# Nine added GpSimd drains near the ends of five stages of a seven-stage transformer block

## The reference

```python
h = layer_norm(concat([meta, x]), ln_in_g, ln_in_b)
proj = h @ w_in                        # 8 + 2*2 + 3*8 heads of 64, and 8 forget logits
o_a = sliding_sink_attention(qa, ka, va, sinks, rel_bias)      # windows of 128 frames, 8 heads
o_b = forgetting_attention(qb, kb, vb, log_sigmoid(fb + b_f))  # causal, 8 heads
h = layer_norm(2 ** 0.25 * h + concat([o_a, o_b]) @ w_o, ln1_g, ln1_b)
ffn = hierarchical_moe(h, ...)         # 1 of 4 groups, 2 of its 8 experts, SwiGLU of width 512
out = layer_norm(2 ** 0.25 * h + ffn, ln2_g, ln2_b)[16:]
```

## Time and profile before

| what | value |
|---|---|
| median of 3 runs | 2470.27 us (2469.62 to 2470.92) |
| the profiled execution | 2470.16 us, of which its span is 2468.5 us |
| busy, share of the span | PE 89%, PEld 72%, DVE 69%, ACT 60%, POOL 13% |
| POOL instructions counted as busy | 429, 324.4 us |
| DMA packets from GpSimd's queue (q0) | 31648, 101.89 MB, 14.3% of 16 engines' span |
| granted TensorE clock, mean | 0.947 |

### The profile page before, as it was taken

One profiled execution on the slowest core, in us unless ns is written; L12 is line 12 of the kernel. 1 busy time (PEld: TensorE's weight loads), 2 busy tenths in 40 slices (PEclk: granted clock), 3 DMA queues, 4 the chain that ended last, 5 costly groups with the idle time before them and its releaser, 6 DMA issues. The chain is left out here.

```text
span 2468.5 us, 35853 instructions
## 1 busy us (share of the span) xinstructions
PE 2192.7 (89%) x11294; PEld 1786.4 (72%) x11294; DVE 1709.2 (69%) x3150; ACT 1489.7 (60%) x2262; POOL 324.4 (13%) x429
## 2 busy tenths in 40 slices
PE   6999999678699989999899993799999999999970
PEld 5788888555477777777778872687888888788860
DVE  5323231288588887888643336898999999899976
ACT  4323241176577676777643330777888888788856
POOL 0112111100000000000000000222222222222211
PEclk9999999889899999999999995899999999999985
DMA  6536252533341222222043323897887969999837
GB/s 197 177 107 198 102 183 81 152 79 96 109 116 32 53 67 66 62 69 75 20 139 136 137 110 136 298 376 242 275 291 214 302 203 363 321 296 304 270 73 289
DMA packets 220553, 420.61 MB, mean 170 GB/s; under 512 B 47912, under 2 KB 97144, under 8 KB 219288
## 3 DMA queue, kind: packets, MB, share of 16 engines
q1 hardware_dynamic: 187760, 316.08, 37.9%
q0 software_dynamic: 31648, 101.89, 14.3%
q10 hardware_dynamic: 1040, 1.31, 0.2%
HBM read 437.68 MB, written 86.39 MB: 212 GB/s over the span
## 5 line engine op out<-in xcount | busy, mean ns | idle before, releaser
L2425 DVE TENSOR_TENSOR moe_w_lo<-fetch_w_raw,moe_w_hi 128x1024 fp32r<-128x1024 f32 x376 | 435.5, 1218 | 14.3 <-ACT moe_w_hi L2354 14.0
L2354 ACT ACTIVATE moe_w_hi<-fetch_w_raw 128x1024 fp32r<-128x1024 f32 x376 | 369.1, 1053 | 70.8 <-PEq L96 32.4
L2479 PE MATMUL moe_ps_gu<-moe_w_hi,moe_xT_hi 128*128 128x512 f32 x736 | 293.8, 399 | 4.3 <-DVE moe_xT_lo L2436 4.2
L2481 PE MATMUL moe_ps_gu<-moe_w_hi,moe_xT_lo 128*128 128x512 f32 x736 | 289.3, 393 | 0.0
L2480 PE MATMUL moe_ps_gu<-moe_w_lo,moe_xT_hi 128*128 128x512 f32 x736 | 289.0, 393 | 0.0
L1434 ACT ACTIVATE fox_p_hi<-fox_ps_t 128x512 fp32r<-128x512 f32 (+4 forms) x352 | 181.0, 530 | 108.7 <-PE fox_ps_t L1574 107.7
L1501 DVE TENSOR_TENSOR fox_p_lo<-fox_ps_t,fox_p_hi 128x512 fp32r<-128x512 f32 (+4 forms) x352 | 211.0, 611 | 28.9 <-ACT fox_p_hi L1434 28.1
L1574 PE MATMUL fox_ps_t<-ident,fox_s 128*128 128x128 f32 (+1 forms) x1216 | 199.8, 279 | 29.6 <-ACT fox_s L1427 18.8
L2431 DVE TENSOR_TENSOR moe_d_lo<-fetch_d_raw,moe_d_hi 128x1024 fp32r<-128x1024 f32 x184 | 213.1, 1221 | 10.5 <-ACT moe_d_hi L2362 7.2
L1488 DVE CUSTOM_DVE_ANT_0 fox_s<-fox_ps_r,fox_ncum 128x512 f32<-128x512 f32 (+4 forms) x352 | 193.6, 569 | 20.8 <-PE fox_ps_r L1559 13.5
L1427 ACT ACTIVATE fox_s<-fox_s,fox_ntop 128x144 f32<-128x144 f32 (+5 forms) x192 | 173.3, 904 | 48.0 <-DVE fox_ntop L1496 47.6
(11 more groups left out here) (319 smaller groups left out, 4978.8 us busy)
## 6 DMA issues: line engine op xcount, KB each, us to landing
fetch_w_raw<-in_w_e_gate_dram SPq DMA_DIRECT2D x192, 512.0 KB
fetch_w_raw<-in_w_e_up_dram SPq DMA_DIRECT2D x192, 512.0 KB
fetch_d_raw<-in_w_e_down_dram SPq DMA_DIRECT2D x92, 1024.0 KB
ahead_raw<-in_w_in_dram SPq DMA_DIRECT2D x24, 1024.0 KB, 5.2
gates_wide<-in_x_dram SPq DMA_DIRECT2D x16, 512.0 KB
h<-gates_wide POOLq DMA_DIRECT2D x16, 512.0 KB, 3.3
gates_wide<-qT SPq DMA_DIRECT2D x32, 256.0 KB, 4.1
mix_h<-h SPq DMA_DIRECT2D x16, 512.0 KB, 3.7
```

The costliest lines, as they stand in the source:

```text
L2354: nc.scalar.activation(w_hi[:, k], w_raw[:, k].rearrange("p j n -> p (j n)"), ACT.Copy).then_inc(gu_high, 1)
L2425: nc.vector.tensor_tensor(w_lo[:, k], w_raw[:, k].rearrange("p j n -> p (j n)"), w_hi[:, k].bitcast(F32), ALU.subtract).then_inc(gu_split, 1)
L2479: nc.tensor.matmul(out, xT_hi[:, slot, k], w_hi[:, k, cols], start=k == 0, stop=False)
L2481: done = nc.tensor.matmul(out, xT_lo[:, slot, k], w_hi[:, k, cols], start=False, stop=k == KT - 1)
```

## The change

Nine calls of `nc.gpsimd.drain()` are added to GpSimd's programs, in five of the seven stages. A drain has no semaphore; it stands in GpSimd's order in front of the store named, and nothing else is moved.

```diff
@@ phase_project
                 for i in range(QK):
+                    if sb == SBS - 1 and i in (QK - 4, QK - 1):
+                        nc.gpsimd.drain()
                     store_chunk(sb, i)
@@ phase_window
+                if n in (TILES // 2, TILES - 1):
+                    nc.gpsimd.drain()
                 pool.wait_ge(o_ready, 2 * (n + 1))
@@ phase_mix
             def store(n, slot, use):
+                if is_tile(n, TILES - 2, TILES - 1):
+                    nc.gpsimd.drain()
                 pool.wait_ge(h1_scaled, n + 1)
@@ phase_combine
             def store(n, slot, use):
+                if n == TILES - 4:
+                    nc.gpsimd.drain()
                 pool.wait_ge(ready, n + 1)
```

## The result

| | before | after |
|---|---|---|
| median of the runs, us | 2470.6 (2469.62 to 2472.69, 4 runs) | 2449.79 (2448.41 to 2452.5, 4 runs) |
| the profiled execution, us; its span | 2470.16; 2468.5 | 2448.41; 2446.8 |
| GpSimd's drains at the ends of the seven stages, us in sum | 17.40 | 1.31 |
| mean granted clock | 0.947 | 0.949 |

The ratio is 0.9916 with an interval of 0.9899 to 0.9933: about 20.8 us less, where 15.6 were forecast.

A forecast was written before the change was run, and what follows sets the result against it. Seven serial stages end in barriers that wait for GpSimd's drains, 17.397 us in all. Ends gain 16.0 us, less 0.4 for first transfers: 15.6 off 2470.16 gives 2454.5; range 2451.5 to 2458.2, or to 2461 with the first rival.

The forecast's parts named there:

- The end drains: Ends of five stages: GpSimd's drains walk only transfers issued since the last drain, falling from 17.12 to 1.10 us.
- rival 2: Stage ends: semaphore clearing, not the drain, empties the list, so end drains keep their length; 2472 us, chance 0.08.
- rival 1: Stage ends: about 1.36 us is a fixed price of a drain behind any transfer; gain 10.3 us, 2459.8, chance 0.11.
- The cover of the added drains: Before the last stores: new drains' walks fit into GpSimd's idle waits and cost nothing; longest 6.5 us, in the projection.
- Rival 3: Added drains: walking beside working engines is far slower than in an empty stage; 2480 us at factor 5, chance 0.08.
- The rule of the Trainium skill: Added drains: GpSimd and VectorE lock each other out of a shared port, making the factor 5 and the result 2480.
- The first transfers behind a drain: Four last stores right behind new drains, on the path: each costs 0.1 us more, 0.4 us in all.
- The last stage: Only place without cover: tile 12's store up to 2.4 us late, the last two on time; cost taken as 0.
- it should move forward rigidly: After each barrier the next stage starts from its own loads and keys, fetched before, so it shifts without changing length.
- at most 2 to 3 us for the clock: Around 493 to 509: a pause 6.8 us shorter may leave fewer slow-clock microseconds; extra gain put into the lower bound alone.
- The prediction's low end, 2451.5: Range's lower bound: 2453.3 if only 46 ns of each drain remained and first transfers cost nothing, plus a little clock gain.

The follow-up runs named there:

- the second's 15.8: The changed kernel, unchanged, run again for more rounds against the kernel before: 2452.09 us against 2468.52, ratio 0.9936 (0.9920 to 0.9952).

## Why the prediction was right and where it failed

- **The end drains.** Right in mechanism and size: 16.07 us against 16.02. The drain in the middle empties the list, and the clearing of semaphores isn't needed for it, so rival 2 falls; the ends of 0.12 to 0.38 us rule out the floor of rival 1.
- **The cover of the added drains.** Right in its result; mis-sized in the walk. The prediction took 108 entries at 60 ns, 6.5 us, for the projection's first drain. It lasts 8.9 us from the end of the issue in front (452.87) to its own end (461.76), 82 ns for each: the 60 ns were 7.01/116, and at this price the end drain doesn't walk all 116. (The 49 ns of the experts were mis-sized in the same way.) Chunk 9 goes out at 462.25; it was due at 457.24 (the old 457.81, less 0.57 by which the stage ran ahead), so it is 5.0 us late instead of 2.2, and GpSimd is back in step at chunk 11 (468.12). That the walk runs beside the landing, as the prediction let it, holds there: the wait for chunk 9 is 9.38 us in all three profiles with this drain, though the landing in front of it takes 3.8, 3.5 and 3.2 us. Where the landing is the longer it doesn't quite hold, and a part of the walk stands behind the last landing: 0.41 us before tile 8 of the windows, 1.19 before tile 14 of the mixing, 0.54 in the last stage and 3.81 in the experts, the same to 0.01 us in three profiles each, and about half of what 9, 28, 12 and 92 entries make at 83 ns. The waits had room for it: in the experts 8.4 us of 13.20 were used.
- **Rival 3** falls with it: the walk costs 82 to 83 ns for each transfer beside working engines and 82 to 85 in the empty stage, a factor of 1; set against the prediction's 6.5 us it is 1.4, where 4.2 would have used up the gain. The rule of the Trainium skill that stood beside it ("SBUF — State Buffer", section "A bandwidth-pool intuition that's wrong (but worth ruling out)") would have made 32 us of the 6.5, as an estimate, 5 times as much; no run here shows that.
- **The first transfers behind a drain.** Mis-sized: 0.4 us was taken, and the stores behind the added drains take 0.53 to 0.55 us, and the two scatters 1.54 and 1.55, no more than before (0.539 and 1.543). Nothing was lost.
- **The last stage.** Right: tile 12 is late (3.2 us, 2.4 at most were forecast), the last two stores are on time.
- **The step that failed: "it should move forward rigidly", with at most 2 to 3 us for the clock.** The bodies of two executions differ by up to 6.2 us in the experts (853.3 to 859.5) and 4.1 in the windows (176.1 to 180.2), in kernels that do the same there. The prediction took the profile of before, 2470.16 us, as the level and three runs that agreed within 1.3 us as the spread; 27 runs spread over 11.2, with a median of 2468.52. That profile has the longest experts' body of ten, by two pauses of TensorE and the clock behind them; why VectorE was late there in some executions and not in others is open. The prediction's low end, 2451.5, held the walks and a little of the clock, and nothing for this. A second term was left out: the 0.83 us of the projection's last store.
- By the parts that come back, the change is worth 16.9 us; the first comparison's 20.8 and the second's 15.8 lie on either side. That the rest of the 20.8 is the spread of the bodies fits all ten profiles; with so few runs a systematic gain of a microsecond or two beside it is not excluded.

Some 1.05 us of walks is left in the five end drains, and no experiment points to a version that would be faster by an amount that can be measured.

## What to carry to other kernels

Where a stage ends with a barrier, look at the drain of each engine under the line that leaves it, not only at busy times: GpSimd's grows with the transfers that it has issued since its last drain, and a drain put where GpSimd waits anyway takes that off the path, if it fits into the wait: 82 to 85 ns for each transfer walked here, and up to half of that behind the landing of the store in front. Take the price from stages whose drains agree on it (three did, two did not). Count the gain by parts that come back from profile to profile, and put the spread of the remaining stages, from more than one profile of the kernel before, into the range.

## What the runs showed that was not expected

- Each transfer that GpSimd issued and that is still on the list costs its next drain 82 to 85 ns, long after it has landed, whether most of them moved 128 and 256 KB (projection, 82 and 83) or all 512 KB (last stage, 85), and whether the other engines work (82 and 83) or have finished.
- The list can shrink without a drain: 128 stores of the forgetting attention leave 1.365 us, 32 leave 0.229; in the projection 108 are walked by a drain before chunk 9 (8.9 us), but the end drain behind 116 takes 7.01.
- A TensorE pause of 3.14 us in the experts' loop goes with 6.83 us at the 1.2 GHz level, one of 1.47 us with 3.41; such pauses come and go between executions of kernels that are the same in that stage, and with them some microseconds of its length.
- A drain anywhere between the projection's stores lets the last of them go out 0.83 us earlier, up to 290 us later (4.37 in place of 5.20 us of waiting).
